# Conditioning product in plain float32 on four column groups, and 32 gate chunks moved from the merge to the projection

## What is computed

```python
mod = jax.nn.silu(c) @ lp['w_ada'] + lp['b_ada']            # c: 9 rows; w_ada: 2048 x 12288
sh1, sc1, g1, sh2, sc2, g2 = jnp.split(mod[:, None, :], N_MOD, axis=-1)
h = x * (1.0 + sc1) + sh1
q, k, v, u, ga, gb = jnp.split(h @ lp['w_in'], cuts, axis=-1)
...
merged = jax.nn.sigmoid(ga) * (att @ lp['w_att_br']) + jax.nn.sigmoid(gb) * (y_s @ lp['w_ssm_br'])
x = _layernorm(DN_ALPHA * x + (1.0 + g1) * (merged @ lp['w_out']), lp['ln1_g'], lp['ln1_b'])
```

## Time and profile before

| what | us |
|---|---|
| median of the 3 runs | 2674.21 (2668.91 to 2675.73) |
| the profiled execution | 2669.05 |
| its span in the profile | 2667.4 |
| opening stage, until VectorE has modulated h | 0 to 264.0 |
| projection, until VectorE reads the first transposes of `projT` | 264.0 to 630.7 |
| attention, state space branch, glu | 630.7 to about 1155 |
| merge, and the first product of w_out | 1155 to 1515.6 |
| the rest of w_out, layer norms, feed-forward, output | 1515.6 to 2667.4 |

### The profile page before, as it was taken

One profiled execution on the slowest core, in us unless ns is written; L12 is line 12 of the kernel. 1 busy time (PEld: TensorE's weight loads), 2 busy tenths in 40 slices (PEclk: granted clock), 3 DMA queues, 4 the chain that ended last, 5 costly groups with the idle time before them and its releaser, 6 DMA issues.

```text
span 2667.4 us, 43491 instructions
## 1 busy us (share of the span) xinstructions
PE 2311.8 (87%) x15405; PEld 2067.2 (77%) x15405; DVE 1458.5 (55%) x1975; ACT 926.2 (35%) x1104; POOL 225.8 (8%) x531
## 2 busy tenths in 40 slices
PE   4565999998777663599999997999999999999997
PEld 2243788886555452499999895999999999999995
DVE  4998666664334344244444546665466546645665
ACT  2323555552333300233333223443233223323323
POOL 0370000001111101100000002000011001000101
PEclk9667999999888856799999998899999999999999
DMA  7545988885666532455555562354655455455441
GB/s 237 194 172 174 286 277 277 279 282 193 239 252 253 185 102 75 135 150 144 155 149 143 149 161 71 111 145 126 169 147 154 119 166 155 116 159 155 137 128 52
DMA packets 579759, 451.54 MB, mean 169 GB/s; under 512 B 15954, under 2 KB 506418, under 8 KB 579362
## 3 DMA queue, kind: packets, MB, share of 16 engines
q1 hardware_dynamic: 569931, 431.44, 53.6%
q0 software_dynamic: 3136, 10.20, 1.1%
q10 hardware_dynamic: 6624, 9.02, 1.1%
HBM read 432.26 MB, written 18.34 MB: 169 GB/s over the span
## 4 chain that ended last, share of the span: by engine, by line
PE 76%; DVE 11%; DMA 4%; issue 3%; ACT 2%; SPq 2%; ACTq 1%; POOL 0%; DVEq 0%; POOLq 0%; PEldq 0%
PE bank L908 16%; PE bank L910 16%; PE bank L909 16%; PE bank L1146 4%; PE bank L1144 4%; PE bank L1145 4%; PE bank L855 2%; PE bank L856 2%; DVE wL L1529 2%; DMA kpage<-in_cache_k 2%; PE bank L1011 1%; PE bank L1082 1%; PE bank L961 1%; PE bank L828 1%; DMA taps_d<-o_s 1%
## 5 line engine op out<-in xcount | busy, mean ns | idle before, releaser
L1529 DVE TENSOR_TENSOR wL<-ring,wH 128x2048 fp32r<-128x2048 f32 (+3 forms) x304 | 625.0, 2064 | 312.5 <-ACT wH L1209 311.7
L1209 ACT ACTIVATE wH<-ring 128x2048 fp32r<-128x2048 f32 (+3 forms) x304 | 509.8, 1687 | 450.8 <-PE bank L910 307.4
L908 PE MATMUL bank<-hH,wH 128*128 128x320 f32 x1920 | 599.1, 312 | 18.3 <-DVE hL L2022 17.3
L910 PE MATMUL bank<-hH,wL 128*128 128x320 f32 x1920 | 596.4, 311 | 0.0
L909 PE MATMUL bank<-hL,wH 128*128 128x320 f32 x1920 | 596.4, 311 | 0.0
L908 PEld LDWEIGHTS bank<-hH,wH 128*128 128x128 f32 x1920 | 362.7, 189 | 28.9 <-issue 14.0
L909 PEld LDWEIGHTS bank<-hL,wH 128*128 128x128 f32 x1920 | 363.4, 189 | 1.5
L910 PEld LDWEIGHTS bank<-hH,wL 128*128 128x128 f32 x1920 | 363.2, 189 | 0.0
L855 PE MATMUL bank<-wH,cHL 128*18 128x512 f32 x384 | 165.2, 430 | 83.7 <-DVE wL L1529 83.6
L908 PE MATMUL bank<-fH,wH 128*128 128x320 f32 x704 | 220.7, 314 | 11.2 <-DVE fL L2055 11.2
L909 PE MATMUL bank<-fL,wH 128*128 128x320 f32 x704 | 219.9, 312 | 0.0
(11 more groups left out here) (391 smaller groups left out, 3374.0 us busy)
## 6 DMA issues: line engine op xcount, KB each, us to landing
ring<-in_w_ada SPq DMA_DIRECT2D x96, 1024.0 KB, 5.2
ring<-in_w_up SPq DMA_DIRECT2D x88, 1024.0 KB, 5.8
ring<-in_w_in SPq DMA_DIRECT2D x64, 1024.0 KB, 6.6
kpage<-in_cache_k SPq DMA_DIRECT2D x64, 512.0 KB, 5.6
vpage<-in_cache_v SPq DMA_DIRECT2D x64, 512.0 KB, 5.8
ring<-in_w_down SPq DMA_DIRECT2D x32, 768.0 KB, 5.0
ring<-in_w_down SPq DMA_DIRECT2D x32, 640.0 KB, 4.5
ring<-in_w_out SPq DMA_DIRECT2D x16, 1024.0 KB, 5.9
```

The costliest lines, as they stand in the source:

```text
L908: t.matmul(acc, a[:, k, :], high[:, k, :], start=(k == 0), stop=False)
L910: last = t.matmul(acc, b[:, k, :], high[:, k, :], start=False, stop=(k == K - 1))
L1209: a.activation(high[:, front:K, :], ring[cc][:, front:K, :], ACT.Copy).then_inc(S["hi_done"], 1)
L1529: v.tensor_tensor(wL[buf][:, front:K, :], ring[cc][:, front:K, :], wH[buf][:, front:K, :].bitcast(F32), SUB)\
```

## The change

- **Units in plain float32.** The conditioning vectors stay float32: `c_cols`, zeroed by GpSimd, has 32 columns for each of the 16 steps, 9 of them in use. A unit is four matmuls (after's L865) straight from the ring slot, each with 32 stationary columns and into its own 32 rows of bank 2 (`k * QUAD`), so on its own group of the array's columns. Nothing of a unit is split any more. `unit_done` and `unit_landed` replace the shared counters. `ada_rows` has 128 rows, and `add_up` (three additions of pieces of `ident`) adds the four groups in the small matmuls.
- **VectorE's opening stage** has no splits. `ada_out` of blocks 0 to 3 comes after the parameter transposes and after every 20th small step.
- **Projection.** Sixteen passes of four times unit, chunk; the 32 gate chunks follow the 32 chunks of u, q, k, v. Chunk weights have two slots of their own, `pring`, at the place of `b1` to `c2`, so the first load waits for `p_stored` and `w_flipped`. There are two pairs `wH`, `wL`, and no half splits.
- **Gates** leave the projection through ScalarE's sigmoid into one of four `gate` tiles; GpSimd stores them in `gates_d` in DRAM. GpSimd, and VectorE ahead of `proj_turns`, wait for all these stores.
- **Merge.** Eight passes of four chunks with K = 1024; SP loads a gate tile behind each weight block. VectorE multiplies, adds and splits each row at once into `mH`, `mL`. The splits for merge and w_out run ahead through glu and merge without a break.

The diff, cut to its core:

```diff
+    pring = [at(f"pring{i}", [P, KD, P], r_vtok + i * KD * P * 4) for i in range(2)]
+    c_cols = at("c_cols", [P, KD, QUAD], r_small2)
+    gates_d = nc.dram_tensor("gates_d", (2 * KD, P, T), F32).ap()
...
-    stages = [("glu", GLU, KA // 4, [KA] * 4), ("merge", MERGE, KD, [KD, KA, KD, KA]),
+    stages = [("glu", GLU, KA // 4, [KA] * 4), ("merge", MERGE, KD // 2, [KA] * 4),
@@ sync
+            def load_proj(n, s, column):
+                sp.wait_ge(S["split_done"], n + (1 + RING - 2))
+                alone(sp)
+                sp.dma_start(pring[s][:], w_in_d[:, :, ds(column, P)]).then_inc(pring_landed[s], 16)
...
-            def proj_pass(i, column):
-                for x, (kind, m) in enumerate(items):
-                    if kind == "unit":
-                        load_unit(i * ITEMS + (PROJ + x), x % RING, i * 2 + (2 * UNITS + m // UNITS), m % UNITS)
-                    else:
-                        load(i * ITEMS + (PROJ + x), x % RING, KD, w_in_d[:, :, ds(column + m * P, P)])
+            def proj_pass(i, column, first=False):
+                for m in range(4):
+                    load_unit(i * UNITS + (UNITS1 + m), m, i + 2 * UNITS, m)
+                    if first and m == 0:
+                        sp.wait_ge(S["p_stored"], 16 * BATCHES)
+                        sp.wait_ge(S["w_flipped"], 1 + BATCHES)
+                    load_proj(i * 4 + (PROJ + m), m % 2, column + m * P)
...
+            with sp.Fori(0, KD // 2) as i:
+                for cc in range(4):
+                    load(i * 4 + (MERGE + cc), cc, KA, (w_ssm_d if cc % 2 else w_att_d)[:, :, ds((i * 2 + cc // 2) * P, P)])
+                    sp.wait_ge(acc_free[cc % 2], i * 2 + (nth_pair(MERGE) + cc // 2))
+                    alone(sp)
+                    sp.dma_start(gate[cc][:], gates_d[ds(i * 2 + (cc // 2 + cc % 2 * KD), 1)].rearrange("o p t -> (o p) t")).then_inc(gate_landed[cc], 16)
@@ gpsimd
+            with pool.Fori(GATES // 4, GLU // 4) as i:
+                for m in range(4):
+                    pool.wait_ge(acc_free[m % 2], i * 2 + (m // 2 + 2))
+                    alone(pool)
+                    pool.dma_start(gates_d[ds(i * 4 + (m - GATES), 1)].rearrange("o p t -> (o p) t"), gate[m][:]).then_inc(gate_stored[m], 16)
@@ tensor
-                for k in range(BLOCK // P):
-                    c = cHL[:, unit * (BLOCK // P) + k, :]
-                    t.matmul(rows, c, wide(wH[buf])[:, k, :], start=(unit == 0 and k == 0), stop=False)
-                    last = t.matmul(rows, c, wide(wL[buf])[:, k, :], start=False, stop=(unit == UNITS - 1 and k == BLOCK // P - 1))
-                last.then_inc(S["chunk_done"], 1)
+                for k in range(UNITS):
+                    last = t.matmul(bank[2][k * QUAD:(k + 1) * QUAD, :], c_cols[:, unit * UNITS + k, :], wide(ring[s])[:, k, :],
+                                    start=(unit == 0), stop=(unit == UNITS - 1))
+                last.then_inc(S["unit_done"], 1)
...
+            with pe.Fori(0, GLU // 4) as i:
+                for m in range(4):
+                    ada_unit(m, i * 16 + (UNITS1 // RING * 16 + 16), i + 2 * UNITS, m)
+                    product(i * 4 + m, m, KD, i * 2 + m // 2, hH, hL, (S["h_ready"], 0) if m == 0 else None)
+                ada_turn(i + 2 * UNITS)
@@ scalar
+                    if gates:
+                        if not first:
+                            act.wait_ge(gate_stored[m], i * 16 - GATES // 4 * 16)
+                        a.activation(gate[m][:], bank[m % 2][:, 0:T], ACT.Sigmoid).then_inc(acc_free[m % 2], 1)
@@ vector
-                if steps[0] % 8 == 0:
+                if steps[0] % 20 == 0:
                     piece()
...
+            for m in range(4):
+                dve.wait_ge(gate_stored[m], 16 * (2 * KD // 4))
             read_turns(proj_turns())
...
-            for k in range(KD):
-                own.step(v.tensor_copy(mH[:, k, :], merged[:, k, :]))
-                v.tensor_tensor(mL[:, k, :], merged[:, k, :], mH[:, k, :].bitcast(F32), SUB).then_inc(S["m_ready"], 1)
+            def merge_pass(i, next_ks):
+                for cc in range(4):
+                    h = cc // 2
+                    dve.wait_ge(S["chunk_done"], i * 4 + (MERGE + cc + 3))
+                    dve.wait_ge(gate_landed[cc], i * 16 + 16)
+                    dve.wait_ge(S["m_ready"], i * 2 + (h + 1))
+                    v.tensor_tensor(part[cc % 2][:], bank[cc % 2][:, 0:T], gate[cc][:], MUL).then_inc(acc_free[cc % 2], 1)
+                    split_ahead(i, MERGE, cc, next_ks, ks_of["merge"])
...
```

More of the change, by code:

```diff
@@ L1130, in _ @@
             pe.wait_ge(S["s_ready"], KA)
-            operands = [(hH, hL), (attH, attL), (hH, hL), (sH, sL)]
-            pe.sem_inc(S["half_done"], 1)
-            with pe.Fori(0, KD) as i:
-                for x, (cc, k0, more) in enumerate(pieces_of_merge):
-                    (a, b), (high, low) = piece_buffers(x), operands[cc]
-                    if more:
-                        pe.wait_ge(S["half_split"], i * 2 + (cc // 2 + 1))
-                    else:
-                        pe.wait_ge(S["split_done"], i * 4 + (MERGE + cc + 1 + RING))
-                    if k0 == 0:
-                        pe.wait_ge(acc_free[cc % 2], i * 2 + (nth_pair(MERGE) + cc // 2 + 1))
-                    acc = bank[cc % 2][:, 0:T]
-                    for k in range(KA):
-                        t.matmul(acc, a[:, k, :], high[:, k0 + k, :], start=(k0 == 0 and k == 0), stop=False)
-                        t.matmul(acc, a[:, k, :], low[:, k0 + k, :], start=False, stop=False)
-                        last = t.matmul(acc, b[:, k, :], high[:, k0 + k, :], start=False, stop=(not more and k == KA - 1))
-                    last.then_inc(S["half_done" if more else "chunk_done"], 1)
-            passes(pe, "out", None, 0, lambda i, _: [products(i, OUT, cc, KD, mH, mL, (S["m_ready"], 0) if cc == 0 else None) for cc in range(4)])
+            operands = [(attH, attL), (sH, sL)]
+            passes(pe, "merge", None, 0, lambda i, _: [products(i, MERGE, cc, KA, *operands[cc % 2]) for cc in range(4)])
+            passes(pe, "out", None, 0, lambda i, _: [products(i, OUT, cc, KD, mH, mL, (S["m_ready"], 1) if cc == 0 else None) for cc in range(4)])
             def layer_norm(nth):
@@ L1272, in _ @@
             ssm_pass(UNITS, first=True)
-            with act.Fori(UNITS + 1, 2 * UNITS - 1) as i:
+            with act.Fori(UNITS + 1, 2 * UNITS) as i:
                 ssm_pass(i)
-            ssm_pass(2 * UNITS - 1, last=True)
-            for x in range(2):
-                split_high(PROJ + x, x, KD, PROJ // RING)
             for name in ("w1_stored", "taps_stored", "p_stored"):
@@ L1971, in residual @@
+            dve.wait_ge(S["s_ready"], KA)
+            passes(dve, "merge", own, 4, merge_pass)
             def residual(src, m, gain, ready, free=None, r=res[0]):
```

305 lines of the change are left out of this document (109 added, 196 removed).

## The result

The kernel after the change takes 2576.47 us (median of 4 runs, 2566.39 to 2579.15), the kernel before beside it 2673.24 us (2668.91 to 2675.73): a ratio of 0.963, with a 95% interval of 0.9598 to 0.9661. It is 97 us faster. The forecast was 2570, in a range of 2538 to 2608. The profiled execution took 2574.98 us, its span is 2573.3 us, 94.1 less than before; the forecast sum was -102.

The account below looks back on a forecast made before the run. TensorE's own work bounds projection and merge; in the opening stage VectorE's chain and the arrival of blocks count. Terms -31 + 169 - 240 = -102 us give 2567 from the profiled execution, 2572 from the median; forecast 2570, range 2538 to 2608.

Parts of the forecast that it names:

- the projection: Projection stage, from 366.7 us before to 535.6 after, so +169 us, with TensorE never idle.
- merge and w_out: Merge and first product of w_out, from 360.8 us to 121, so -240 us, with merge pairs at 7.0 to 7.1 us.
- the opening stage: Everything up to the start of modulate: the two halves together give 31 us, from 0 to 55.
- Unit in the projection: Projection: a unit of four float32 matmuls on four column groups takes 0.98 us, ends 0.89 and 1.10.
- third rival: Projection bound by its loads (+46 us, 2616) or paying for the change of form (51 us, 2621); chance 0.10 for both.
- The tail: End of the projection: the last gate passes ScalarE, GpSimd's issue and its store before VectorE may read, 5 us.
- Opening stage, first half: To VectorE's last parameter step: steps start at 39.5 and end at 99 instead of 111.3, gain 12 us, between 4 and 36.
- Opening stage, second half: From VectorE's last parameter step to the start of modulate: 108 us instead of 127, gain 19, ends 89 and 128.
- Gates through DRAM: Projection and merge: gate stores fit beside the weight loads, merge gate loads are behind nobody; the last gate costs 5 us.
- little (half of it gone): Rival: in the opening stage, VectorE's new waits and GpSimd use up half and more of the gain, 2590 to 2601; chance 0.13.
- second rival: Opening stage gives more, by store pace from the first batch or VectorE hardly waiting for blocks: 2540 to 2550; chance 0.12.
- The groups do not run one after another: Rival claiming they do, in the projection: a unit takes 3.4 us, +155 us, 2725; chance 0.03.

## Why the prediction was right, and where its sum was off

The forecast named the right bound in every stage. The sum, -102 against -94, is made of errors of both signs: the projection is 12.6 us worse than reckoned, merge and w_out 2.4, the opening stage about 6 better. That it came so near is in part luck.

- **Merge and w_out: right.** -240 forecast, -237.6 measured. A pair takes 7.04 us, forecast 7.0 to 7.1. VectorE's multiplications, two pairs and then the first product of w_out:

```profile
1309.64 0.49 DVE L1883 TENSOR_TENSOR part<-bank,gate 128x320 f32<-128x320 f32 x1 [1.20 <-PE bank L914]
...
1316.68 0.49 DVE L1883 TENSOR_TENSOR part<-bank,gate 128x320 f32<-128x320 f32 x1 [1.20 <-PE bank L914]
...
1323.72 0.49 DVE L1883 TENSOR_TENSOR part<-bank,gate 128x320 f32<-128x320 f32 x1 [1.20 <-PE bank L914]
...
1423.83 0.48 DVE L1898 TENSOR_SCALAR res<-bank,mod 128x256 f32<-128x256 f32 x1 [3.00 <-PE bank L914]
```

  The 5.53 us of waiting for `mL` are gone, and the wait for the first w_out split is 1.09 us, forecast about 1. Of the 2 us that are missing, 1.5 are the merge's first product: its matmuls stand 0.27 us apart at first (lower clock), and it takes 4.99 (1300.93 to 1305.92) where 3.52 were reckoned.
- **Unit in the projection: mechanism right, size off.** The step that failed is "I take 0.98 us for a unit", with the upper end at 1.10. A unit and its chunk take 8.23 us (500.96 to 509.20), so a unit with what it does to its neighbours costs 8.23 - 7.04 = 1.19 us, beyond that end. The 0.98 came from the earlier trace rows, the distance from the start of L1014 to the start of what follows. It held the wait inside the unit's own length, but not the slow first step of what follows nor the slow last step of what stands ahead. The kernel before already had that last one: the prediction ends the last chunk at 402.95 while the small matmuls start at 403.04, and booked the 0.09 to the small matmuls. The prediction had the right idea in its third rival and drew a wrong conclusion ("0.98 us has one change of form in it"): 0.21 us for each unit were missing. 63 x 0.21 = 13.2 us, of which the small matmuls gave back 4: behind the last chunk of a pass they stand in the place of one change of form, their own way in is no slow step any more now that they have 128 rows (499.93 to 500.08), and a pass has only 0.79 us for them (33.71 - 4 x 8.23) where 1.07 was reckoned.
- **Two smaller terms of the projection.** The first chunk ran at the lower clock for its first half and took 9.9 us (229.63 to 239.55): 2.9 not reckoned, since all 64 were priced at full clock. The tail took 5.6 us, forecast 5. The chunks are 7.04 and not 7.03, 0.6 for all. With the units that is 13.2 - 4.2 + 2.9 + 0.6 + 0.6 = 13.1 us, against 12.6 from 535.6 to 548.2; the terms as they are written add up to 535.0 to 535.3, so it closes within 0.2.
- **Opening stage, first half: right sum, wrong start.** The steps started at 50.04, forecast 39.5. The prediction let the transposes follow "as soon as their sources have landed, about 32"; c_raw lands at 38.3 (in the run with log_dt's own semaphore) and log_dt, whose load takes 7.6 us to issue, at 41.4. But VectorE's end hangs on block 3: its wait ended at 78.74 and 21 us of steps were left, forecast 78 and 21. So the late start shows as less standing, 13.6 us instead of 24. The 10 us were not simply hidden. While TensorE stood for log_dt the ring filled up and its loads paused, so that the edit for log_dt brought the end forward as well. Slices of 2.75 us from the start on, the two low ones of the pause at 46.75 to 52.25:

```profile
GB/s 27 51 147 392 265 293 347 304 262 342 339 239 333 344 378 421 340 89 12 313 386 392 386 390 385 390 384 390 384 387 364 18 0 0 0 0 0 0 6 191
```

  The end of the wait was thus right by two errors that cancel: the loads ran at 384 to 392 GB/s behind that pause, forecast 350.
- **Opening stage, second half: 6.6 us better than forecast.** The stretching by GpSimd is shown by the run with GpSimd nearly idle; TensorE's low clock beside it is a second part that the run doesn't separate. A batch beside GpSimd took 13.3 us on average (112.02 to 178.27 for five), forecast 14.5 for four and 10 for the fifth, which is 1.8 less in all. The last three took 7.7 us each with the last block in them, forecast 8.9 and 2 for the block: 5.6 less. The forecast's terms add up to 108.7 and not 108, the rest of the distance.
- **Gates through DRAM: right.** They cost the last store and nothing else.
- **The rivals.** The opening stage gave 36.9 us where the sum had 31: neither little (half of it gone) nor as much as the second rival (20 to 30 more). The projection is not bound by its loads, but the second half of that rival, the change of form, came true at a quarter of its price. The groups do not run one after another.
- **Slips in the prediction's arithmetic** that change no reading: 8.4 MB at 286 GB/s end the steps at 104 and not 107, the pace of the stores throughout gives 85 and not 89, and half of the opening stage's gain gone would be 2586 and not 2590.
- **Not explained:** +1.3 us in attention to glu and -2.3 behind w_out. Nothing was changed there, and the runs differ by more.

## What to carry to other kernels

Narrow float32 products on four column groups give four matmuls for the price of one, and need no splits: here 0.89 us for four of 512 columns. Put them side by side, since each way in and out of that form cost 0.3 us here, which a busy engine shows only as a slower first and last step of its neighbours. When work is moved to where the loads have room, the store and reload of a result can be free, as the 10.5 MB were here, as long as the last one isn't next in line; put the tiles that travel first. And where an engine waits for arrivals in a chain of its own work, read the arrival times from the trace and put each use behind them.

## What the runs showed of the hardware

- Four float32 matmuls of 128x32 by 512 on four column groups: 0.89 us in a row of sixteen, 1.00 alone, 3.55 when all four go to one group. That is 3.6 to 4.0 times. The Trainium skill has 2.38 times for three column tiles ("TensorE: Matmul & The Clock Gate", Measured speedup vs the span model); the runs here are better than that scaled to four (3.2).
- A change between four groups and the whole array shows as 0.10 us at each side, in steps that otherwise take 0.147, and the weight load behind it isn't done ahead. Matmuls with 18 stationary columns and 128 rows, before the change, showed no such step.
- A sustained load of blocks of 1 MB, half of them with rows of 512 B, ran at 291 GB/s over 390 us and at 311 over 100 us with 98% of the DMA engines busy.
- VectorE's addition of two tiles of 128x1024 takes 1.23 us alone and 2.83 to 5.06 beside GpSimd's element work, the latter with two of GpSimd's instructions in its time.
- The broadcast load of log_dt, 32 KB to 128 partitions, held ScalarE's queue for 7.6 us and landed 21.4 us after its issue, beside other loads. The same load held it for 5.8 us and landed in 11.7 in the kernel before, so this is no fixed price.
